# Weight splits two tiles ahead of TensorE in the state-space groups, in place of three

## The reference, cut to what matters

```
scores = (C B^T) * exp(cum_q - cum_k + log dt)      # lower triangle, or upper
y      = scores x                                   # both directions summed
y      = rmsnorm((y + d * x) * silu(z)) @ w_out     # w_out: 2048 x 1024
```

## Time and profile before

| | us |
|---|---|
| median of 3 runs | 1822.18 (1821.94 to 1822.78) |
| the profiled execution | 1822.79 |
| its span | 1821.0 |
| PE busy in the span | 1744.6 (96%) |
| DVE busy | 1080.4 (59%) |
| ACT busy | 887.8 (49%) |
| POOL busy | 117.4 (6%) |

### The profile page before, as it was taken

How to read it: one execution, slowest core, us unless ns; L and a number is a source line. 1 busy time by engine, 2 the same in 40 slices (tenths; PEclk the granted TensorE clock), 3 DMA queues, 4 the chain that set the end, 5 groups by cost and what they waited for, 6 DMA issues and landing times.

```text
span 1821.0 us, 23181 instructions
## 1 busy us (share of the span) xinstructions
PE 1744.6 (96%) x9432; PEld 1475.2 (81%) x9432; DVE 1080.4 (59%) x1432; ACT 887.8 (49%) x1227; POOL 117.4 (6%) x85
## 2 busy tenths in 40 slices
PE   7999899996779999999999999999999999999998
PEld 5888799994557888888888768888889888888886
DVE  4554477987655654575555685554665455576643
ACT  4443456655335443564444565444553444545532
POOL 0000000000000000000001430000000134200000
PEclk9999899998889999999999999999999999999999
DMA  7655576755324655586655505655565523356552
GB/s 254 186 184 175 156 189 186 201 184 134 100 58 145 185 185 175 172 217 221 202 185 184 174 1 179 203 185 173 185 197 163 161 71 94 128 172 196 185 175 80
DMA packets 244073, 300.58 MB, mean 165 GB/s; under 512 B 9344, under 2 KB 175616, under 8 KB 243968
## 3 DMA queue, kind: packets, MB, share of 16 engines
q1 hardware_dynamic: 238608, 289.78, 50.5%
q10 hardware_dynamic: 5360, 9.32, 2.2%
HBM read 297.96 MB, written 1.11 MB: 164 GB/s over the span
## 4 chain that ended last, share of the span: by engine, by line
PE 93%; DVE 4%; ACT 2%; issue 1%; DMA 0%; SPq 0%; DVEq 0%; POOL 0%; ACTq 0%
PE bank L506 89%; PE bank L509 4%; DVE EW L1849 1%; DVE wlo L1641 1%; ACT whi L1179 1%; DVE EW L1641 1%; DMA h<-in_x 0%; ACT hThi L1179 0%; ACT EW L1176 0%; ACT xn L1176 0%; DVE bc L1644 0%; DVE cbm L1641 0%; DVE hTlo L1644 0%; DVE h L1644 0%; DVE xn L1644 0%
## 5 line engine op out<-in xcount | busy, mean ns | idle before, releaser
L1641 DVE TENSOR_TENSOR wlo<-raw,whi 128x2048 fp32r<-128x2048 f32 (+2 forms) x272 | 593.2, 2186 | 379.9 <-ACT whi L1179 379.9
L1179 ACT ACTIVATE whi<-raw 128x2048 fp32r<-128x2048 f32 (+2 forms) x284 | 518.1, 1831 | 289.8 <-PE bank L506 285.0
L506 PE MATMUL bank<-whi,hThi 128*128 128x512 f32 x1072 | 426.9, 398 | 2.1 <-DVE wlo L1641 2.1
L506 PE MATMUL bank<-wlo,hThi 128*128 128x512 f32 x1072 | 419.6, 391 | 0.0
L506 PE MATMUL bank<-whi,hTlo 128*128 128x512 f32 x1072 | 405.1, 392 | 0.1
L506 PE MATMUL bank<-hThi,whi 128*128 128x256 f32 (+1 forms) x912 | 262.9, 288 | 1.4 <-ACT hThi L1179 0.8
L506 PE MATMUL bank<-hTlo,whi 128*128 128x256 f32 (+1 forms) x912 | 259.8, 285 | 0.0
L506 PE MATMUL bank<-hThi,wlo 128*128 128x256 f32 (+1 forms) x912 | 259.7, 285 | 0.0
L506 PEld LDWEIGHTS bank<-whi,hThi 128*128 128x128 f32 x1072 | 202.7, 189 | 45.3 <-issue 2.5
L506 PEld LDWEIGHTS bank<-whi,hTlo 128*128 128x128 f32 x1072 | 202.4, 189 | 44.5 <-DVE hTlo L1644 1.5
L506 PEld LDWEIGHTS bank<-wlo,hThi 128*128 128x128 f32 x1072 | 202.8, 189 | 40.1
(11 more groups left out here) (200 smaller groups left out, 1997.1 us busy)
## 6 DMA issues: line engine op xcount, KB each, us to landing
raw<-in_ffn_w_gu SPq DMA_DIRECT2D x172, 512.0 KB, 4.9
raw<-in_ffn_w_down SPq DMA_DIRECT2D x40, 1024.0 KB, 5.0
raw<-in_w_in SPq DMA_DIRECT2D x30, 1024.0 KB, 5.2
raw<-in_ssd_w_in SPq DMA_DIRECT2D x16, 1024.0 KB, 5.6
raw<-in_ssd_w_in SPq DMA_DIRECT2D x32, 512.0 KB, 5.4
raw<-in_w_up SPq DMA_DIRECT2D x16, 1024.0 KB, 5.4
raw<-in_w_down SPq DMA_DIRECT2D x16, 1024.0 KB, 5.0
raw<-in_na_w_qkv SPq DMA_DIRECT2D x12, 1024.0 KB, 5.2
```

The lines of the kernel that those rows point to most:

```text
L506: return T.e.matmul(out, lhsT, rhs, start=start, stop=stop, skip_group_check=skip)
L1179: return e.activation(out, in_, ACT.Identity, **kw)
L1641: return e.tensor_tensor(out, a, b, op)
```

## The change

In the loop over the eight state-space groups ScalarE and VectorE call `take("yout", g, hold=1)`, so that there the new split is that of tile n+1, and it waits for TensorE's last use of tile n-2. In round 0 nothing is left to split, since tile `yout, 1` was split in the projection. The next `take`, that of `pproj, 0, 0`, which has no hold, then splits two tiles (`up, 1, 0, 0` and `up, 1, 0, 1`) where it split one. ScalarE's `ple_load(0)` comes after `take("yout", 7)` and no longer before it, and SP's `pos(0)` comes one tile earlier.

```diff
         for n in range(2, len(plan.tiles)):
-            if n == tile["yout", 7] + 6:
+            if n == tile["yout", 7] + 5:
                 pos(0)
@@ scalar, ssd()
                 columns_of(g)
-                if g == 7:
-                    ple_load(0)
-                take("yout", g)
+                take("yout", g, hold=1)
+            ple_load(0)
             high(2, 0, 0)
             high(2, 0, 1)
             take("pproj", 0, 0)
```

## The result

| | before | after |
|---|---|---|
| median, us | 1822.06 (1820.5 to 1822.78) | 1788.86 (1788.06 to 1789.86) |
| ratio, 95% interval | | 0.9819 (0.9802 to 0.9836) |
| the profiled execution | 1822.79 | 1789.86 |
| its span | 1821.0 | 1788.0 |
| PE busy in the span | 1744.6 (96%) | 1731.6 (97%) |

The kernel is 33.2 us faster; 31.6 were forecast (1790.6, range 1789.0 to 1795.0).

What follows compares the result with a forecast made beforehand. In the state-space groups a loop of waits was the bound, closed by ScalarE's split waiting for a buffer TensorE held. Gains of 30.53 us to the end of `outputs(7)` and 1.05 in the tail gave 1790.6 us, range 1789.0 to 1795.0.

Steps and rivals of the forecast that it cites:

- The wait in rounds 1 to 6: State-space rounds: with the hold the split's buffer is already free, so rounds of 19.9 to 20.4 us become 15.47.
- Round 0 and the sum to the end of outputs(7): Round 0 has no split, gaining 4.04 us; with the shorter rounds, 30.53 us gained to the end of `outputs(7)`.
- The tail: From `outputs(7)` to the first `up` matmul: of a 2.03 us wait about 1.05 gained; bounds -1 to +2.
- The moved steps: `pos(0)`, later loads of tiles +5 and +6, and rows of sums: all covered by slack, costed at nothing.
- The clock: TensorE's gap before the squares shrinks from 5.73 to 3.4 us, so squares and output tile run at full clock.
- the first rival: TensorE's gap before the squares still drops the clock; the last round gives back 2.71 us: 1793.3 us, chance 15%.
- Total: Whole kernel: 31.6 us gained, 1790.6 us; TensorE passes the gain on whole after the stage.
- Rival 2: VectorE's round is longer than read, operations 3% longer beside busy TensorE plus waits: 5.4 us lost, 1796; chance 14%.
- Rivals 3 and 4: Split waits for something else: 1818 to 1822 us, 3%; TensorE stays at 1.2 GHz: near 1843, 2%.

Runs made afterwards that it cites:

- x1: The changed kernel, but in round 7 ScalarE and VectorE take without the hold, as before; 1792.2 us, ratio to before 0.9836.
- x5: Changed kernel, ScalarE's split put ahead of `columns_of`, low splits of yout,2 to yout,7 on GpSimd, started after VectorE's product with the gate; 1790.0 us.
- x4: The kernel before, with 18 additional matmuls in TensorE's gap ahead of the squares in rounds 2 to 6; 1809.71 us, ratio 0.9933.

## Why the prediction was right

- *The wait in rounds 1 to 6* was right: a round of 15.47 us read from round 0 and 1, 15.47 or 15.48 us measured, in all five intervals between the decays of rounds 1 to 6. Round 0 had shown the loop without its wait, so that no duration had to be guessed.
- *Round 0 and the sum to the end of outputs(7)*: 30.53 us forecast, 30.57 measured (551.15 - 520.58).
- *The tail*: 1.05 forecast. 31.62 less 30.57 is 1.05, and x1 gave 1.06.
- *The moved steps* cost nothing. `pT` landed later than forecast and held ScalarE for 1.03 us, where it had 7.21 us to spare afterwards.
- *The clock* was wrong as a mechanism; that it cost nothing was luck in part. I expected a clock of 1.00 from the second round on. It fell in the output tiles whose squares begin at 433.00, 463.96 and 494.90; with the squares they took 8.1 us, where the others took 6.6: the first rival's mechanism, in three of six tiles. In all but the last tile TensorE's slack covered that. The last tile happened to run at the full clock. The trace of x1, with the same loop, shows that no strict alternation stands behind it:

```profile
464.16 1.03 PE L506 MATMUL bank<-gate,cst 128*2 128x128 f32 x8 [1.94 <-DVE EW L1640]
472.28 1.47 PE L506 MATMUL bank<-bc 128*128 128x256 f32 x8
```

The tile before this one was slow too (8.07 us), the gap was short, and the clock fell all the same, so that this tile took 8.12 us. The rival's price was too high as well: 2.71 us was read behind gaps of 5.73 us, where the clock was low before the squares began. A fall in the last tile costs 1.6 us in x5; with it the forecast would have been 1792.2 and not 1793.3. The chance of 15% was too small for a mechanism that came in half of the tiles.

- *Total*: 1.7 us lower than forecast. The profiled executions show where: from the first `up` matmul to the end it took 1248.86 us before and 1247.48 after, 1.4 us that no step of mine held. Nothing there was changed, so these came by luck; where they lie is shown at the end.

Rival 2 (a longer VectorE round beside a busy TensorE) is out: the decays take 4.18 to 4.20 us in all kernels without work on GpSimd. Rivals 3 and 4 are out by the result.

## What to carry to other kernels

Depth of prefetch is no good in itself: with three buffers, splitting three tiles ahead means that each split waits for the buffer in use, and puts that wait into two engines' queues. Look for the round in which the buffer happens to be free; it gives the time of the loop without the wait. Then ask what is next in the loop: here it was an order on ScalarE, worth another 9.65 us once the buffer was free, and nothing before. A split moved to an idle GpSimd is not free for VectorE: in three placements one of its instructions on SBUF stood until GpSimd's had ended.

## What the runs showed of the hardware that was not expected

**The clock can fall after TensorE has restarted.** Busy time by microsecond of the changed kernel, around TensorE's gap from 460.5 to 463.96:

```profile
463.00:464.00 1.00, 0.04 (x1) 0.07 (x2) 1.00 (x3) 0.00 (x0) 0.00 (x0) 1.00 0.29 90
464.00:465.00 1.00, 1.00 (x9) 0.63 (x9) 1.00 (x3) 0.00 (x0) 0.00 (x0) 1.00 0.54 162
465.00:466.00 1.00, 1.00 (x3) 0.81 (x4) 1.00 (x4) 0.00 (x0) 0.00 (x0) 0.52 0.90 350
...
469.00:470.00 1.00, 1.00 (x6) 0.83 (x5) 0.00 (x0) 1.00 (x1) 0.00 (x0) 1.00 0.00 0
```

TensorE had been at work again for a microsecond at full clock, and only then the clock fell to 0.50, some 4.5 us after TensorE had stopped; by the earlier trace rows it fell some 4.1 us after the stop at 451.2. That the next work starts before that point therefore doesn't save it: this was the flaw in my argument. Nor is there one length of gap that decides: one of 2.10 us (at 433.0) and that of 1.94 in x1 were followed by a fall too, ones of 1.86 and 1.89 were not, one of 3.19 in x5 (ahead of 463.26) was not, and a gap of 2.03 us went either way, in x4 and in the kernel before. The rule of the Trainium skill, "TensorE: Matmul & The Clock Gate" (Part 1: The HAM clock gate), that the monitor's window runs freely agrees with this.

**Identical code takes 2 to 3 us more or less.** `products(1)` begins at 407.99 to 411.12 us in the ten profiled executions, with the same instructions ahead of it, and from the first `up` matmul to the end it takes 1247.0 to 1249.0. In one place the cause can be seen. Busy time by stretch, before and then after, around the same matmuls:

```profile
1430.00:1446.00 16.00, 14.09 (x83) 12.18 (x81) 3.63 (x4) 8.64 (x10) 4.55 (x1) 0.79 0.62 195
```

```profile
1398.00:1414.00 16.00, 14.09 (x93) 12.14 (x92) 4.47 (x6) 9.51 (x10) 4.57 (x1) 0.89 0.63 197
```

Much the same work had a granted clock of 0.79 in the one and 0.89 in the other: the low clock lasted half as long. Two marks on TensorE's timeline, before and then after, give its worth:

```profile
1434.74 1.51 PE L506 MATMUL bank<-qk 64*128 64x256 f32 x4 [1.91 <-DVE fgT L1641]
1441.59 0.98 PE L506 MATMUL bank<-qk 64*128 64x256 f32 x4
```

```profile
1403.37 1.34 PE L506 MATMUL bank<-qk 64*128 64x256 f32 x4 [1.91 <-DVE fgT L1640]
1408.79 0.92 PE L506 MATMUL bank<-qk 64*128 64x256 f32 x4
```

From the one to the other it took 6.85 us and then 5.42: 1.43 us, the 1.4 that the forecast lacked in the profiled execution. It is one execution each; that such differences make up the whole scatter is not shown. For effects near a microsecond, a stretch between two marks in the trace tells more than the medians do.
